# Chunk attention with its probabilities and values as upper and lower fp32r halves, from the fourth row tile on

## The chip, the cores and the metric

The kernel runs on one core of a Trainium2 chip (trn2). The metric is the device time of one execution in microseconds (us). Five engines have in-order instruction streams of their own and meet at semaphores: TensorE (PE: weight loads, PEld, and matmuls), VectorE (DVE), ScalarE (ACT), GpSimd (POOL) and SyncE (SP, which issues loads).

## The reference

Two transformer blocks on 1024 tokens of 1024 channels, fp32. The part that matters is one of three attentions of the second block:

```python
def _chunk_rel(q, k, v, rel_table):        # 4 heads of 64, chunks of 64 rows, 8 chunks to the left
    ...
        kb = lax.dynamic_slice_in_dim(kp, start, BAND, axis=1)
        vb = lax.dynamic_slice_in_dim(vp, start, BAND, axis=1)
        valid = (start - pad + ki) >= 0
        sc = jnp.einsum('bqhd,bkhd->bhqk', qc, kb, preferred_element_type=jnp.float32) * scale
        sc = jnp.where(valid, sc + bias[None], -jnp.inf)
        p = jax.nn.softmax(sc, axis=-1).astype(vb.dtype)
        return jnp.einsum('bhqk,bkhd->bqhd', p, vb)
```

## The kernel before

Products are made in one of two ways. In most of them each fp32 operand is split into an upper half rounded to fp32r and a lower half (the rest), and three fp32r matmuls are added up: helper lines L495 to L497. The products of probabilities and values, and the transposes, are plain fp32 matmuls.

**Chunk attention.** Eight row tiles i of 128 rows, four heads h each: 32 heads in a row, numbered x = 4i + h, in a software pipeline of iterations `it` (`class Heads`, `class Chunked`). Row tile i sees min(i+1, 5) key blocks of 128, so 128, 256, 384, 512 and then always 640 keys. In iteration `it`, in this order,
- PE computes the scores of head `it` (fp32r, keys in two halves, L2963), transposes the probabilities of head `it`-2 (one fp32 matmul against the identity for each key block, L2977; blocks 0 to 3 go to one PSUM bank, block 4 to the other of two "turn" banks, 4 and 5, which are handed out in turn), and multiplies the transposed probabilities of head `it`-3 with the values (L2989, one fp32 matmul for each key block, 64 columns of output, into bank 6 or 7).
- ACT copies its share of transposed groups of head `it`-2 from PSUM (`copy_turned`, L3023), then makes the exponential of head `it` with its sum (L3045); where `it`-3 is the last head of a row tile, it squares that tile's output for a later normalization (L3061).
- DVE copies its share of the transposed groups (L3021), adds the bias to the scores and takes the extreme of each row (negated, so it is a minimum, L3109), and at the end of a row tile takes the reciprocal of the sums (L3077), multiplies them onto the value sums in PSUM (L3081), and one iteration later scales the normalized output (L3125), for which POOL has made the root (L577, L570).

`claim` makes PE wait until the engine that reads a PSUM bank has released it. `turns_by_dve(x, g)` says which of DVE and ACT copies group g of head x: for odd x DVE takes the first group and ACT the second, for even x the other way round. The transposed probabilities and the row tile outputs sit in SBUF: two buffers `pt2` (heads x and x+2 share one), one buffer `o2`.

**The values.** Eight tiles of 128 tokens x 256 channels, `cv`. Five are computed ahead of the stage (`CV_EARLY`), three inside it, in iterations 0 to 2, by 24 fp32r matmuls each; ACT copies each from PSUM (`cv_copy_act`, L3176). ACT also rounds the next stages' weights (L455, `send_to`) in iterations 3 and 6. Behind the stage comes the narrow projection, 24 fp32r matmuls of 420 columns for each of eight token tiles.

## Time and profile before

| | |
|---|---|
| runs of the kernel before | 2338.84 us median of 3 (2338.25 to 2340.36) |
| the profiled execution | 2341.6 us, span 2339.8 us |
| TensorE clock granted | 0.997 of full |
| chunk attention | 1110.9 to 1176.0 us from the span's start |

Times in the timeline are from the span's start. "Idle before <- X" names what ended an idle stretch. Matmul records overlap, since each lasts until its last column has left the array: what a matmul costs in a row of them is the distance of the starts. An fp32 matmul shows as two records. In the profile fp32r matmuls are written "f32" as well.

### The profile page before, as it was taken

What the parts mean: (1) busy time and instruction counts of PE and PEld (TensorE: products, weight loads), DVE (VectorE), ACT (ScalarE), POOL (GpSimd) and SP (SyncE); (2) the same over time, 40 slices, a digit from 0 to 9 for tenths busy, and PEclk for the clock granted to TensorE, in tenths of its full rate; (3) what the DMA queues carried; (4) which work ended last, traced back from release to release, by engine and by line L of the source; (5) the groups of instructions that cost most, each with busy time, mean ns of one, the idle gap of its engine ahead of it and who ended that gap; (6) DMA issues with size and microseconds to landing.
All of it is one profiled execution on the core that took longest, in us unless ns stands there. A gap on an engine that the chain in (4) does not pass through costs nothing. (4 is left out here: it accounts for less than half of the span.)

```text
span 2339.8 us, 30722 instructions
## 1 busy us (share of the span) xinstructions
PE 2303.4 (98%) x11602; PEld 1943.8 (83%) x11602; DVE 1427.8 (61%) x2217; ACT 967.7 (41%) x1965; POOL 863.9 (37%) x733
## 2 busy tenths in 40 slices
PE   9999999999999999999999999999999999999998
PEld 8788888888888888888998877888888888888887
DVE  7999924955454577775533767153494545447776
ACT  4126534533332345455635655134453233234543
POOL 2000125388787800032113121122338878770002
PEclk9999999999999999999999999999999999999999
DMA  5222124233233368664002100243223323336865
GB/s 158 52 63 77 51 90 131 86 117 117 86 117 104 117 243 284 212 215 120 19 19 70 46 5 19 64 154 126 87 67 117 117 86 117 104 120 247 285 214 191
DMA packets 219444, 275.84 MB, mean 118 GB/s; under 512 B 17243, under 2 KB 144956, under 8 KB 216482
## 3 DMA queue, kind: packets, MB, share of 16 engines
q1 hardware_dynamic: 200594, 210.57, 29.0%
q10 hardware_dynamic: 18704, 63.32, 6.9%
q8 instruction: 92, 1.51, 0.3%
q14 instruction: 54, 0.44, 0.1%
HBM read 205.27 MB, written 68.57 MB: 117 GB/s over the span
## 5 line engine op out<-in xcount | busy, mean ns | idle before, releaser
L495 PE MATMUL P<-ah,wh 128*128 128x512 f32 (+1 forms) x1136 | 441.4, 389 | 0.2 <-DVE al L525 0.2
L497 PE MATMUL P<-ah,wl 128*128 128x512 f32 (+1 forms) x1136 | 439.1, 387 | 0.0
L496 PE MATMUL P<-al,wh 128*128 128x512 f32 (+1 forms) x1136 | 439.0, 386 | 0.0
L495 PE MATMUL P<-wh,ah 128*128 128x512 f32 (+2 forms) x1128 | 425.8, 377 | 0.0
L497 PE MATMUL P<-wh,al 128*128 128x512 f32 (+2 forms) x1128 | 423.6, 376 | 0.0
L496 PE MATMUL P<-wl,ah 128*128 128x512 f32 (+2 forms) x1128 | 423.2, 375 | 0.0
L577 POOL TENSOR_TENSOR stats<-stats,epsc 128x1 f32<-128x1 f32 x78 | 32.6, 417 | 773.0 <-ACT xn L1895 421.0
L495 PEld LDWEIGHTS P<-ah,wh 128*128 128x128 f32 x1136 | 213.5, 188 | 43.3 <-issue 0.4
L497 PEld LDWEIGHTS P<-ah,wl 128*128 128x128 f32 x1136 | 213.4, 188 | 43.4
L496 PEld LDWEIGHTS P<-al,wh 128*128 128x128 f32 x1136 | 213.6, 188 | 42.2
L497 PEld LDWEIGHTS P<-wh,al 128*128 128x128 f32 x1128 | 212.3, 188 | 36.5
L496 PEld LDWEIGHTS P<-wl,ah 128*128 128x128 f32 x1128 | 212.4, 188 | 36.3
L495 PEld LDWEIGHTS P<-wh,ah 128*128 128x128 f32 x1128 | 212.4, 188 | 36.2
L461 POOL TENSOR_TENSOR wl<-stage,wh 128x1024 fp32r<-128x1024 f32 (+3 forms) x43 | 99.3, 2316 | 303.1 <-ACT wh L455 302.8
L2819 POOL TENSOR_TENSOR wl<-ws,wh 128x512 fp32r<-128x512 f32 x154 | 203.9, 1346 | 3.0
L2819 POOL TENSOR_TENSOR wl<-stage,wh 128x512 fp32r<-128x512 f32 x128 | 181.5, 1433 | 49.9 <-DVE al L525 34.5
L2352 ACT ACTIVATE wh<-ws 128x512 fp32r<-128x512 f32 x160 | 96.5, 627 | 193.8 <-POOL ws L2812 189.4
L1188 DVE SCALAR_TENSOR_TENSOR acc<-hp,cwt,acc 128x1024 f32<-128x1024 f32 (+1 forms) x142 | 153.1, 1120 | 1.3
L2504 ACT ACTIVATE ah<-rf 128x512 fp32r<-128x512 f32 x154 | 95.7, 622 | 66.4 <-DMA rf<-ff_rows 63.6
L2712 DVE TENSOR_TENSOR al<-rf,ah 128x512 fp32r<-128x512 f32 x154 | 105.6, 686 | 18.7 <-ACT ah L2504 18.4
L455 ACT ACTIVATE wh<-stage 128x1024 fp32r<-128x1024 f32 (+2 forms) x68 | 68.8, 1015 | 78.0 <-PE P L497 49.6
L2352 ACT ACTIVATE wh<-stage 128x512 fp32r<-128x512 f32 x132 | 79.8, 621 | 45.3 <-PE P L497 30.2
(362 smaller groups left out, 4303.2 us busy)
## 6 DMA issues: line engine op xcount, KB each, us to landing
rf<-ff_rows SPq DMA_DIRECT2D x154, 256.0 KB, 5.4
stage<-in_w_down_dram SPq DMA_DIRECT2D x110, 256.0 KB, 3.8
ff_rows<-sb ACTq DMA_DIRECT2D x22, 1024.0 KB, 5.0
stage<-in_w_gu_dram SPq DMA_DIRECT2D x44, 512.0 KB, 5.2
stage<-in_w_in_dram SPq DMA_DIRECT2D x22, 512.0 KB, 4.0
stage<-in_w_gate_dram SPq DMA_DIRECT2D x22, 512.0 KB, 4.6
stage<-in_w_up_dram SPq DMA_DIRECT2D x22, 512.0 KB, 5.1
ff_rows<-uo ACTq DMA_DIRECT2D x22, 512.0 KB, 3.0
```

The source lines that it names most:

```text
L455: e.activation(WH[n % RING][:, 0:plan[n][0]], stage[place(n)][:, 0:plan[n][0]], ACT.Copy).then_inc(*wh.up(n))
L461: port.e.tensor_tensor(WL[n % RING][:, 0:w], stage[place(n)][:, 0:w], WH[n % RING][:, 0:w].bitcast(F32), ALU.subtract).then_inc(*sig.up(n))
L495: e.matmul(out, lh, rh, start=start, stop=False, skip_group_check=onto)
L496: e.matmul(out, lh, rl, start=False, stop=False, skip_group_check=onto)
L497: return e.matmul(out, ll, rh, start=False, stop=stop, skip_group_check=onto)
L577: PL.e.tensor_tensor(v, s, more, ALU.add).then_inc(*rs.up((key, "v")))
L1188: e.scalar_tensor_tensor(dst, src, cwt[:, c, w:w + 1], dst, ALU.mult, ALU.add).then_inc(*tap.up(key))
L2352: AC.e.activation(hi, src, ACT.Copy).then_inc(*wh.up((self.name, (m, op))))
L2504: AC.e.activation(self.rows_place(u)[0], RF[b][:, :], ACT.Copy).then_inc(*ah.up((self.name, "split", u)))
L2712: DV.e.tensor_tensor(lo, RF[self.row_buffer(u)[0]][:, :], hi.bitcast(F32), ALU.subtract).then_inc(*al.up((self.name, "split", u)))
L2819: PL.e.tensor_tensor(lo, src, hi.bitcast(F32), ALU.subtract).then_inc(*wl.up((self.name, (m, op))))
```

## The change

- The values are kept in eight tiles `cv0` to `cv7` of [128, 4, 128]: for each head 64 columns of upper halves (ACT's copy, rounded to fp32r) and 64 of lower ones (`cv_low_dve`: DVE subtracts the upper half from PSUM). PE's bank for a value tile is released by DVE (`al`) instead of ACT (`cp`).
- From head 12 on (row tile 3), the first group of transposed probabilities (key blocks 0 to 3) is kept as an upper half, copied by ACT (`pt_hi`), and a lower half, subtracted by DVE after ACT's copy (`pt_lo`). PE's turn bank is released by DVE's subtraction. The group of the fifth key block is always copied by ACT, in fp32.
- A split key block is multiplied by two fp32r matmuls: upper probabilities with both value halves (128 columns), lower probabilities with the upper value half (64 columns). A block that isn't split is one fp32 matmul as before, but with both value halves (128 columns). So the value sums of each head are 128 wide: upper part and lower part.
- At the end of each row tile DVE copies the lower sums from PSUM to `o`, adds the upper ones, and multiplies by the reciprocal: three instructions, each waiting for the one before, where there was one.
- For split heads DVE's order in an iteration is: extreme of head `it`, then the subtraction for head `it`-2 (before: the copy first).

```diff
+        def turned_signal(self, x, g):
+            return ev if self.split(x, g) or self.turns_by_dve(x, g) else cp
+
+        def value_block(self, out, x, h, kb, k, last):
+
+            e = PE.e
+            if not self.split(x, kb - kb % 4):
+                v = self.halves(h, k).bitcast(F32) if self.stacked(x // 4) else self.v(h, k)
+                return e.matmul(out, self.pt(x, kb, 1)[:, 0, :], v, start=kb == 0, stop=last)
+            hi, lo, both = self.pt_hi(x, kb, 1)[:, 0, :], self.pt_lo(x, kb, 1)[:, 0, :], self.halves(h, k)
+            if kb == 0:
+                e.matmul(out, hi, both, start=True, stop=False)
+            ins = e.matmul(out[:, 0:self.dv], lo, both[:, 0:self.dv], start=False, stop=False, skip_group_check=True)
+            if kb:
+                ins = e.matmul(out, hi, both, start=False, stop=last)
+            return ins
...
-                        claim(b, ev if self.turns_by_dve(x, g) else cp, (self.kind, "pt", x, g))
+                        claim(b, self.turned_signal(x, g), (self.kind, "pt", x, g))
...
-                        ins = e.matmul(P[:, b, self.dv * h:self.dv * h + self.dv], self.pt(x, kb, 1)[:, 0, :],
-                                       self.v(h, k0 + kb), start=kb == 0, stop=kb == nb - 1)
+                        ins = self.value_block(P[:, b, n * h:n * h + n], x, h, kb, k0 + kb, kb == nb - 1)
...
+                halved = self.split(x, g)
+                if not halved and (port is DV) != bool(self.turns_by_dve(x, g)):
                     continue
...
+                if halved and port is DV:
+                    DV.wait_ge(cp, (self.kind, "pt", x, g))
+                    DV.e.tensor_tensor(self.pt_lo(x, g, w), src, dst.bitcast(F32), ALU.subtract).then_inc(
+                        *ev.up((self.kind, "pt", x, g)))
+                    continue
...
-                if 2 <= it <= self.n + 1:
+                halved = 2 <= it <= self.n + 1 and self.split(it - 2, 0)
+                if 2 <= it <= self.n + 1 and not halved:
                     self.copy_turned(DV, it - 2)
                 self.turned_dve(it - 1)
                 if it < self.n:
                     self.maximum(it)
+                if halved:
+                    self.copy_turned(DV, it - 2)
...
+                    if self.stacked(i):
+                        both = P[:, 6 + i % 2, :].rearrange("p (h y d) -> p h y d", h=self.nh, y=2)
+                        e.tensor_copy(o, both[:, :, 1, :]).then_inc(*sm.up((self.kind, "lower", i)))
+                        DV.wait_ge(sm, (self.kind, "lower", i))
+                        e.tensor_tensor(o, both[:, :, 0, :], o, ALU.add).then_inc(*sm.up((self.kind, "sum", i)))
+                        DV.wait_ge(sm, (self.kind, "sum", i))
+                        src = o
+                    e.tensor_tensor(o, src, rden.unsqueeze(2).to_broadcast([128, self.nh, self.dv]),
                                     ALU.mult).then_inc(*ev.up((self.kind, "o", i)))
...
+    def cv_low_dve(t):
+        DV.wait_ge(cp, ("cv", t))
+        DV.e.tensor_tensor(cv[t][:, :, 64:128], P[:, cv_bank(t), 0:256].rearrange("p (h d) -> p h d", h=4),
+                           cv[t][:, :, 0:64].bitcast(F32), ALU.subtract).then_inc(*al.up(("cv", t)))
...
+        upper = [big(f"pt2h_{i}", [128, 4, 128], 57.5 + 2.5 * i, F32R) for i in range(2)]
+        lower = [big(f"pt2l_{i}", [128, 4, 128], 2 + 2 * i, F32R) for i in range(2)]
...
+        def split(self, x, g):
+            return x >= 12 and g == 0
+
+        def turns_by_dve(self, x, g):
+            return x < 12 and x % 2
...
+        def turned_dve(self, it):
+            if CV_EARLY <= CV_EARLY + it < NT:
+                cv_low_dve(CV_EARLY + it)
```

## Rows read from the trace of the kernel before

**Rows 1.** The page, busy time (us), share of the span and instructions of an engine.

```profile
PE 2303.4 (98%) x11602; PEld 1943.8 (83%) x11602; DVE 1427.8 (61%) x2217; ACT 967.7 (41%) x1965; POOL 863.9 (37%) x733
```

**Rows 2.** Windows: span, then busy us of PE, PEld, DVE, ACT, POOL; clock, DMA.

```profile
1120.70:1140.00 19.30, 18.39 (x143) 16.71 (x142) 13.70 (x46) 14.88 (x44) 6.82 (x8) 1.00 0.20 56
1140.00:1171.20 31.20, 31.20 (x266) 31.12 (x266) 20.82 (x55) 19.34 (x50) 2.70 (x8) 1.00 0.01 1
```

**Rows 3.** Timeline of PE, one full iteration: start us, us, engine, line, operation.

```profile
1144.28 0.83 PE L2963 MATMUL P<-ck,cqs 128*128 128x320 f32 x4
1144.95 0.71 PE L2977 MATMUL P<-ident,s 128*128 128x128 f32 x5
1145.49 1.23 PE L2989 MATMUL P<-cv,pt 128*128 128x64 f32 x10
1146.53 0.83 PE L2963 MATMUL P<-ck,cqs 128*128 128x320 f32 x4
```

**Rows 4.** Timeline of PE's weight loads around three fp32r matmuls of 128 columns.

```profile
1267.03 0.19 PEld L2966 LDWEIGHTS P<-causal_r,ident_r 128*128 128x128 f32 x1
1267.14 0.19 PEld L2963 LDWEIGHTS P<-fk,fqs 128*128 128x128 f32 x1
1267.25 0.19 PEld L495 LDWEIGHTS P<-ah,wh 128*128 128x128 f32 x1
```

**Rows 5.** Timeline of PE in latent attention, whose values are 128 columns wide.

```profile
1459.99 1.95 PE L2989 MATMUL P<-mv,pt 128*128 128x128 f32 x16
1461.78 0.38 PE L2977 MATMUL P<-ident,p 128*128 128x128 f32 x2
```

**Rows 6.** Groups by form, ACT and DVE: busy us, mean ns, idle before.

```profile
L3023 ACT ACTIVATE pt<-P 128x512 f32<-128x512 f32 x10 | 5.7, 575 | 0.0
L3023 ACT ACTIVATE pt<-P 128x128 f32<-128x128 f32 x10 | 2.7, 266 | 1.6 <-PE P L2977 1.6
L525 DVE TENSOR_TENSOR al<-P,ah 128x512 fp32r<-128x512 f32 x72 | 47.0, 685 | 32.2 <-ACT ah L517 32.2
L525 DVE TENSOR_TENSOR al<-P,ah 128x256 fp32r<-128x256 f32 x16 | 6.8, 423 | 13.3 <-ACT ah L517 13.2
```

**Rows 7.** Timeline of ACT, DVE and POOL at the end of row tile 4.

```profile
1151.26 0.83 ACT L3045 ACTIVATE s<-s,stats 128x640 f32<-128x640 f32 x1 [0.56 <-DVE stats L3109]
1151.35 0.42 DVE L3081 TENSOR_TENSOR o<-P,stats 128x256 f32<-128x256 f32 x1
...
1152.00 0.19 ACT L3045 ACTIVATION_READ_ACCUMULATOR s<-s,stats 128x1 f32 x1
1152.09 0.40 ACT L3061 ACTIVATE yc<-o 128x256 f32<-128x256 f32 x1
...
1152.39 0.19 ACT L3061 ACTIVATION_READ_ACCUMULATOR yc<-o 128x1 f32 x1
...
1152.93 0.55 POOL L570 TENSOR_TENSOR stats<-stats,nhalf 128x1 f32<-128x1 f32 x1
1152.94 0.81 DVE L3109 CUSTOM_DVE_ANT_0 s<-P,b 128x640 f32<-128x640 f32 x1
...
1153.68 0.08 DVE L3109 DVE_READ_ACCUMULATOR2_ANT stats<- 128x1 f32 x1
1153.68 0.48 DVE L3125 SCALAR_TENSOR_TENSOR yc<-o,stats,gout 128x256 f32<-128x256 f32 x1
```

**Rows 8.** Timeline of PE and ACT in row tiles 0 to 3.

```profile
1121.28 0.40 ACT L3045 ACTIVATE s<-s,stats 128x128 f32<-128x128 f32 x1 [0.46 <-DVE stats L3109]
...
1122.78 0.44 PE L2989 MATMUL P<-cv,pt 128*128 128x64 f32 x2 [0.62 <-ACT pt L3023]
...
1124.98 1.04 ACT L455 ACTIVATE wh<-stage 128x1024 fp32r<-128x1024 f32 x1
...
1126.57 0.44 PE L2977 MATMUL P<-ident,s 128*128 128x128 f32 x2 [0.28 <-ACT s L3045]
...
1137.27 1.00 PE L2989 MATMUL P<-cv,pt 128*128 128x64 f32 x8
```

**Rows 9.** Timeline of PE in the last iterations.

```profile
1173.23 0.77 PE L2977 MATMUL P<-ident,s 128*128 128x128 f32 x5 [0.17 <-ACT pt L3023]
```

## What the change will do to the time

> **What bounds the kernel now.** I read the page's busy shares first: TensorE (PE) is busy 98% of the span [rows 1]. Chunk attention takes some 65 us of it. The table by stage shows PE with no idle time from 1140.0 to 1171.2 and 0.9 us of it in the 19.3 us of the narrow tiles before, while VectorE (DVE) is busy 20.8 and ScalarE (ACT) 19.3 of 31.2 us [rows 2]. So a microsecond more or less on PE's path here is one in the total; work on DVE and ACT is free until PE waits for it.
>
> The timeline of PE shows what a full iteration is made of [rows 3]: scores 0.67 us (1144.28 to 1144.95), five transposes 0.54, values 1.04 for ten records, 2.25 together (1144.28 to 1146.53). An fp32 value matmul is two records, so a record takes 104 to 112 ns. "A record" below is a weight load and its matmul.
>
> **What the change does to PE.** Before, 120 value blocks were 240 records. After, the 80 split blocks are two fp32r records each and the 40 others two fp32 records each: 240 again. The question is what a narrow record costs.
> - The moving side does not set it: fp32 values 128 wide in latent attention take 1.79 us for 16 records (1459.99 to 1461.78), 112 ns each [rows 5], like those 64 wide here. So the 40 unsplit blocks, now 128 wide, cost nothing more.
> - The load sets it, for fp32r too: where three fp32r matmuls only 128 wide follow each other, their weight loads start at 1267.03, 1267.14 and 1267.25, 0.11 us apart [rows 4].
>
> I take 112 ns for an fp32r record: change on PE 0. The bounds: 167 ns, what an fp32r score 320 wide takes (0.67 us for four, [rows 3]), would be 55 x 160 = +8.8 us; the low bound is an estimate of 60 ns, a load half as long with a little on top, 52 x 160 = -8.3 us.
>
> The Trainium skill speaks against my value. "TensorE: Matmul & The Clock Gate", Weight-path perf modes, says that fast weight load is on for 128 weights of a type other than FP32, at about twice the speed. If fp32r counted as such, the loads would be halved. By that rule the stage would win what the first rival below says. The trace does not agree: its fp32r loads keep 0.11 us.
>
> **What it does to ACT and DVE.** ACT copies 128x512 in 0.57 and 128x128 in 0.27 [rows 6]; its exponential of 640, the read of the sum with it, takes 0.92 (1151.26 to 1152.19), DVE's minimum with its read 0.82 (1152.94 to 1153.76) [rows 7]. The lower half (transposed probabilities minus the upper ones, PSUM in, fp32r out) is costed by the same form in row passes, 0.69; for 128x256 it is 0.42 [rows 6]. Overlap with the next instruction makes each some 0.08 shorter in a queue; a semaphore costs 0.03 to 0.05.
> - Per head from row tile 3 on, ACT has both copies (about 1.75 us with the exponential), DVE a minimum and a subtraction (1.43). Both fit into 2.25.
> - A new chain: transposes of head x, upper copy, subtraction, and only then may PE transpose head x+1 into the same bank (five key blocks use both turn banks for each head). From the first transpose: 0.60 to the signal (0.71 for five, 0.11 less for four, [rows 3]), 0.62 and 0.73 for copy and subtraction with their semaphores, 0.05 back to PE: 2.00. PE comes back after 2.25. It fits by some 0.25, if both engines are free.
> - Per row tile, DVE finishes the output by a copy of the lower sums, an addition and a multiplication, each waiting for the one before, where it had one multiplication (0.42, [rows 7]). Two more of 0.42 and 0.03: 0.90 us later. Bounds 0.30 (an SBUF source) and 0.48 (the scaling of the same size, [rows 7]) for each. Behind it on DVE wait the next head's minimum and the subtraction; on ACT the square waits for the output, and **behind the square the next head's upper copy**. The old order had cover for one multiplication, not for three.
>
> **A regular tile, walked.** Time from the start of PE's iteration that ends row tile i; T is the head whose transposes come there. T's upper copy 1.30 to 1.87; DVE's minimum 0.87 to 1.69; subtraction 1.91 to 2.60. Value sums ready 2.41. Reciprocal 2.52; copy 2.73; addition 3.18; multiplication 3.63 to 4.05. ACT: square 4.09, free at 4.49; upper copy of T+1 (transposed by 3.52) 4.49 to 5.06. DVE: minimum until 4.79, subtraction 5.10 to 5.79. PE wants to transpose T+2 at 4.49 + 0.67 = 5.16, and can at 5.84: it stalls **0.68 us**. One iteration on, DVE's scaling (its root comes 0.9 us after the square's read, 1152.58 to 1153.48 in [rows 7]) and a minimum end at 6.93, upper copy of T+2 at 7.04, subtraction 7.77, PE due at 8.09: caught up. Nothing accumulates.
>
> **The sum.**
> - In iteration 3 the lower half of the eighth value tile (0.42, in a queue 0.34) goes before the minimum of head 3, for which ACT's exponential is waiting [rows 8]; ACT's next copy is what PE stalls for at 1122.78: +0.34.
> - Row tile 0: PE is idle before 1126.57 for the exponential, which stood behind the square and the 1.04 us weight rounding of 1124.98 [rows 8]; the square is 0.90 later: +0.90.
> - Row tiles 1 and 2: tile 1's 0.90 is mostly covered (0.2 left, but DVE enters tile 2 0.4 late). In tile 2 the iterations are short (1.6 to 1.9 us). From the start of iteration 14 (1132.86, some 0.06 late): DVE's minimum until 1.79; ACT, behind the late exponential of head 13, the upper copy of head 12 until 2.37; its subtraction until 3.10; reciprocal, copy, addition, multiplication until 4.55; square; upper copy of head 13 until 5.56, its subtraction until 6.29, PE at 6.34: the value matmuls of head 13, at 1137.27 before [rows 8], start at 1139.20, +1.93 for both tiles.
> - Row tile 3: as the regular tile, but the iteration has one value block less, so PE is back 0.21 earlier: +0.89.
> - Tiles 4 and 5: 2 x 0.68 = +1.36.
> - Tile 6 and the end: there are no scores left in the iteration that stalls, so PE is back 0.64 earlier, and the last heads run at the chain's own pace. Before, PE idled 0.17 there [rows 9]. Walked to the last value matmul: +1.65. Tile 7's output has the 4.6 us of the next stage's first tile as cover.
> - The other five or so subtractions for value tiles lie under PE's token matmuls: 0.
>
> Sum 7.1 us; PE 0. No DMA moves, no queue of SP or POOL gets anything. Against the profiled execution 2341.6 + 7.1 = 2348.7; that one lies 2.8 above the median of the runs shown, so the forecast is 2338.8 + 7.1 = **2345.9 us**, 0.30% slower. What a measurement can tell from no change is 0.2%, 4.7 us: from 2334.2 to 2343.5.
>
> **Rivals.**
> 1. *Narrow fp32r records at 60 ns instead of 112* (the other side). 8 x 52 ns = 0.42 a head. With five blocks the chain of 2.00 allows only 0.25 of it, 16 heads: 4.0; in tile 3 it is 4 x 0.42 = 1.7. Sum -5.7, net +1.4: 2340.2, not slower. It decides from a saving of 2.4 us, some 0.12 a head. For it: the moving part of 64 or 128 columns is far shorter than 112 ns. Against: the loads of that very type in [rows 4]. 8%, of which 3 end under -0.2% (only if the chain is shorter too). The skill's rule above is this rival.
> 2. *The output chain is covered better*: each added operation 0.30 instead of 0.45 makes every one of seven stalls 0.3 shorter, 7.1 - 2.1 = 5.0; with tile 1 fully covered and the first stall lost in ACT's own waits 7.1 - 3.5 = 3.6: 2342.4, no measurable change. For it: PE's slack of 0.25 an iteration can take back what ACT is late. Against: the regular walk leaves no doubt of order, since all three engines are in order. 20%.
> 3. *The chain does not fit*: semaphores and ACT's fifth-block copy make it 2.45 instead of 2.00. Then PE loses 0.2 in each of 15 iterations and never recovers in a tile: 7.1 + 3.0 = 10.1, 2348.9. For it: the margin is thin beside so many summed durations. Against: each handover in the trace is 0.03 to 0.05. 13%.
> 4. *Narrow fp32r is dearer on PE*, up to the 167 ns bound: up to 7.1 + 8.8 = 15.9, 2354.7. [rows 4] speak against it. 5%.
>
> My forecast (stalls of 5 to 9 us in all): 54%.
>
> **Numbers.** Slower by over 0.2%: 54 + 13 + 5 = 72. Same: rivals 1 and 2 less the fast end, 25. Faster: 3. The range of 2341.0 to 2350.5 takes in rivals 2 and 3 and leaves out rival 1, rival 4 and a few in 100 beyond rival 3's sum; the forecast's own is 2343.5 to 2348.
>
> **What the changed profile would show.** Right: the value matmuls of a head still ten records in about 1.04 us, fp32r loads 0.11 apart; PE idle in front of a transpose, released by DVE's subtraction, once per row tile for 0.5 to 0.9 us and between them none; over 1 us before the values of head 13; ACT's square waiting for DVE's output and the upper copy directly behind it; the next stage starting some 7 us later. Wrong: value groups of 0.6 us (rival 1), idle PE in every iteration (rival 3), value groups over 1.2 us (rival 4), stalls under 0.4 us (rival 2).

## The result, and the profile after

| | before | after |
|---|---|---|
| median of 6 runs | 2339.36 us (2338.25 to 2340.67) | 2351.42 us (2349.41 to 2355.11) |
| ratio | | 1.0052, 95% interval 1.0042 to 1.0062 |
| profiled execution, span | 2341.6, 2339.8 us | 2349.41, 2347.3 us |

The change makes the kernel 12.1 us slower. 7.1 was forecast; the sign is right, the time lies above the range (2350.5).

The page of after, busy times. Beside [rows 1] DVE has 26 and ACT 18 instructions more, PE exactly as many records as before.

```profile
PE 2304.7 (98%) x11602; PEld 1941.6 (83%) x11602; DVE 1442.4 (61%) x2243; ACT 973.4 (41%) x1983; POOL 864.8 (37%) x733
```

The windows of after, same columns as [rows 2]. PE, without idle time from 1140.0 to 1171.2 before, now has 2.3 us of it, and 2.2 in the narrow tiles, where it had 0.9. (The windows don't cover the same heads to the microsecond: after enters the stage 2.4 us earlier.) The last one has no counterpart in the chunk stage of before: a stretch at clock 0.50, 1.2 GHz where the rows around it are at 2.4.

```profile
1120.70:1140.00 19.30, 17.11 (x123) 14.68 (x124) 15.14 (x47) 13.71 (x39) 6.68 (x8) 1.00 0.20 55
1140.00:1171.20 31.20, 28.92 (x240) 27.93 (x238) 24.34 (x54) 21.38 (x58) 2.22 (x6) 1.00 0.01 2
...
1179.40:1186.20 6.80, 6.80 (x31) 6.71 (x29) 2.05 (x5) 1.07 (x3) 0.00 (x0) 0.50 0.00 0
```

The timeline of after, the iteration that ends row tile 4 and the one behind it (all engines but the weight loads). It is the walk of the prediction, in the order that it had.

```profile
1150.95 0.83 PE L2988 MATMUL P<-ck,cqs 128*128 128x320 f32 x4
...
1152.26 0.60 ACT L3054 ACTIVATE pt2h<-P 128x512 fp32r<-128x512 f32 x1 [0.68 <-PE P L3002]
...
1152.99 0.69 DVE L3048 TENSOR_TENSOR pt2l<-P,pt2h 128x512 fp32r<-128x512 f32 x1 [0.33 <-ACT pt2h L3054]
...
1153.20 0.83 PE L2988 MATMUL P<-ck,cqs 128*128 128x320 f32 x4
1153.60 0.17 DVE L3111 RECIPROCAL stats<-stats 128x4 f32<-128x4 f32 x1
...
1153.80 0.42 DVE L3119 COPY o<-P 128x256 f32<-128x256 f32 x1
...
1154.26 0.43 DVE L3121 TENSOR_TENSOR o<-P,o 128x256 f32<-128x256 f32 x1
...
1154.72 0.42 DVE L3124 TENSOR_TENSOR o<-o,stats 128x256 f32<-128x256 f32 x1
...
1155.18 0.42 ACT L3092 ACTIVATE yc<-o 128x256 f32<-128x256 f32 x1 [1.34 <-DVE o L3124]
...
1155.60 0.58 ACT L3054 ACTIVATE pt2h<-P 128x512 fp32r<-128x512 f32 x1
...
1156.27 0.69 DVE L3048 TENSOR_TENSOR pt2l<-P,pt2h 128x512 fp32r<-128x512 f32 x1 [0.39 <-ACT pt2h L3054]
...
1157.02 0.66 PE L3002 MATMUL P<-ident,s 128*128 128x128 f32 x4 [0.73 <-DVE pt2l L3048]
```

The iteration itself still takes 2.25 us (1150.95 to 1153.20), as in [rows 3]. The output now is a chain of three (1153.80 to 1155.14); the square waits for it, the upper copy stands behind the square, the subtraction behind that, and PE idles in front of the transposes: 0.73 us here, 0.82 at 1147.07 and 0.73 at 1166.97 behind the row tiles before and after. The same timeline over the stage, PE's other long stalls:

```profile
1125.38 0.44 PE L3002 MATMUL P<-ident,s 128*128 128x128 f32 x2 [0.58 <-ACT s L3076]
...
1138.16 0.33 PE L2967 MATMUL P<-cv,pt2h 128*128 128x128 f32 x1 [1.10 <-DVE pt2l L3048]
...
1176.91 0.77 PE L3002 MATMUL P<-ident,s 128*128 128x128 f32 x5 [1.31 <-DVE pt2l L3048]
...
1179.08 1.08 PE L3002 MATMUL P<-ident,s 128*128 128x128 f32 x5 [0.29 <-DVE pt2l L3048]
```

The last line is in the half-clock stretch, so its five transposes show 1.08 us. To size the terms I use a second profile of the changed kernel, *again* below, which has no such stretch in or behind the stage.

**Lags.** "Lag" below is how much later a row starts than its counterpart before, both counted from the start of the scores of head 1 (1113.97 us before, 1111.77 in again). Example: the next stage's first transposes start at 1185.46 before and 1193.38 in again, so the lag is 81.61 - 71.49 = 10.12 us.

### The profile page after: what moved, and what is told of

It is laid out like the page before. It is cut to its first block and busy times, and to the rows that moved or that the text cites. A ratio compares the mean times of both kernels' runs of the same rounds, so it can differ in the third digit from the quotient of the medians.

```text
span 2347.3 us, 30788 instructions
## 1 busy us (share of the span) xinstructions
PE 2304.7 (98%) x11602; PEld 1941.6 (83%) x11602; DVE 1442.4 (61%) x2243; ACT 973.4 (41%) x1983; POOL 864.8 (37%) x733
## 5 line engine op out<-in xcount | busy, mean ns | idle before, releaser
L1188 DVE SCALAR_TENSOR_TENSOR acc<-hp,cwt,acc 128x1024 f32<-128x1024 f32 (+1 forms) x142 | 153.1, 1120 | 1.3
```

The costliest lines, as they stand in the source:

```text
L1188: e.scalar_tensor_tensor(dst, src, cwt[:, c, w:w + 1], dst, ALU.mult, ALU.add).then_inc(*tap.up(key))
```

## The experiments

The medians are of 5 runs each, of 11 for one_mult, values_only and no_lower_probs and of 7 for clear. All were timed beside runs of the kernel before on the same chip. "Over before" is against the median of those runs: 2339.72 for again, one_mult, values_only and no_lower_probs; 2338.42 for square_late, both_orders, tail_fill and fixed; 2338.30 for spread, early_loads, all_three and busy_wait; 2338.70 for clear and square_clear. These four groups ran on four chips, so kernels of different groups are compared by this column. The lags are those of one profiled execution each, half-clock stretches included.

| kernel | median us | over before | ratio, 95% interval | lag at last values / next stage's transposes |
|---|---|---|---|---|
| again | 2351.78 | 12.1 | 1.0050 (1.0038 to 1.0063) | 8.89 / 10.12 |
| one_mult | 2343.57 | 3.9 | 1.0015 (1.0006 to 1.0023) | 3.11 / 3.29 |
| values_only | 2343.44 | 3.7 | 1.0014 (1.0006 to 1.0023) | 1.99 / 3.22 |
| no_lower_probs | 2337.97 | -1.8 | 0.9994 (0.9985 to 1.0003) | -4.35 / -3.11 |
| square_late | 2349.60 | 11.2 | 1.0047 (1.0034 to 1.0059) | 9.94 / 10.87 |
| both_orders | 2351.81 | 13.4 | 1.0058 (1.0044 to 1.0071) | 11.43 / 13.35 |
| tail_fill | 2351.41 | 13.0 | 1.0053 (1.0041 to 1.0066) | 8.98 / 9.91 |
| fixed | 2352.68 | 14.3 | 1.0058 (1.0046 to 1.0071) | 10.34 / 11.30 |
| spread | 2348.76 | 10.5 | 1.0042 (1.0028 to 1.0056) | 7.07 / 8.20 |
| early_loads | 2349.89 | 11.6 | 1.0050 (1.0038 to 1.0063) | 8.88 / 9.15 |
| all_three | 2347.15 | 8.8 | 1.0036 (1.0023 to 1.0049) | 7.54 / 7.49 |
| busy_wait | 2352.81 | 14.5 | 1.0058 (1.0045 to 1.0071) | 10.79 / 12.81 |
| clear | 2345.14 | 6.4 | 1.0027 (1.0016 to 1.0037) | 5.21 / 5.15 |
| square_clear | 2349.83 | 11.1 | 1.0040 (1.0026 to 1.0053) | 6.74 / 7.77 |

### Which part costs: again, one_mult, values_only, no_lower_probs

**again** is the changed kernel unaltered.

> The changed kernel once more, unchanged, for a second profile. Theory A (three parts: the output's two more DVE instructions with the square and the next upper copy queued behind them stall PE for about 8.6 us in chunk attention; PE's records cost nothing more; and the idle stretches let TensorE's clock fall to its lower level at the stage's end, which costs some 3 us more): the time is 2351 plus or minus 2 and follows the clock: PE's idle time in the stage is again 8 to 9 us, and what differs between the two profiles is how long the clock is at half. Theory B (no clock part; 12 us are all waits that one profile doesn't show rightly): idle time in the stage near 12 us.

It repeats the result: +12.1 us. The lag in the stage is 8.89 us with no half-clock stretch there, so theory B (12 us of waits in the stage) is out. Whether idle PE brings the clock down is not shown by this run.

**one_mult** takes the output from the upper sums alone, one multiplication as before; it leaves the products with the lower value halves out of the result.

```diff
-                        e.tensor_copy(o, both[:, :, 1, :]).then_inc(*sm.up((self.kind, "lower", i)))
-                        DV.wait_ge(sm, (self.kind, "lower", i))
-                        e.tensor_tensor(o, both[:, :, 0, :], o, ALU.add).then_inc(*sm.up((self.kind, "sum", i)))
-                        DV.wait_ge(sm, (self.kind, "sum", i))
-                        src = o
+                        src = both[:, :, 0, :]
```

> The row tile's output is made by one multiplication of the upper sums, as before; the copy and addition of the lower sums are left out, so the lower halves of the values don't reach the output. Theory A: DVE's output is 0.93 us earlier. By the same walk that leaves 0.34 for the last value tile, about 0.5 in tile 2, under 0.1 in a regular tile and 0.9 at the end: 2341 to 2342, and no stretch at half clock at the stage's end. Rival (the chain of upper copy and subtraction in every iteration, or narrow fp32r records, is what costs): 2347 or more, with PE idle in front of transposes in iterations that end no row tile.

2343.57: 8.2 us less than again, 2 us more than expected. Without the two added operations of DVE on eight row tiles, 0.9 us each, two thirds of the cost are gone. Lag before the transposes of head 7 (their row is [rows 8], 1126.57): 0.33, where again has 1.24. These are the 0.34 and 0.90 of the sum, each within a hundredth; but half of the second shows one wait earlier than forecast, at the values of head 5, which wait 0.35 us for DVE's copy (lag 0.84 there).

**values_only** halves no probabilities: the values stay split and the output is made in three steps.

```diff
         def split(self, x, g):
-            return x >= 12 and g == 0
+            return False
         def turns_by_dve(self, x, g):
-            return x < 12 and x % 2
+            return (x + g // 4) % 2
```

> Only the values are kept in halves: the probabilities are never split, so every value product is one fp32 matmul 128 columns wide, DVE and ACT share the copies as before, and the output still takes three instructions. Theory A: the three instructions are needed for the stall but not enough; without the subtraction behind ACT's copy PE has a copy's time more. Left are 0.34, the 0.9 of tile 0 and some 0.5 in tiles 1 and 2: about 2341.2. Rival 1 (the output chain alone costs it): 2347 or more. Rival 2 (fp32 matmuls 128 wide cost more than 64 wide, 240 records): at 10 ns each 2.4 us more, and value groups of five blocks longer than 1.04 us.

The waits of PE in it, 1120 to 1180 us (us in total, times, longest): none stands in row tiles 3 to 6.

```profile
PE P L2964 <- ACT pt L3054: 0.6, 1, 0.6
PE P L3002 <- ACT s L3076: 0.6, 1, 0.6
PE P L2964 <- DVE pt L3052: 0.4, 1, 0.4
PE P L3002 <- ACT pt L3054: 0.3, 1, 0.3
```

So the three steps do nothing by themselves once iterations are 2.25 us long (lag 1.62 to 1.65 from head 17 to head 26), and the halves do little there (one_mult: 1.40 to 1.62 over the same heads). Only together do they stall PE in the regular tiles, as the walk has it; each of them, taken away alone, takes 8.2 or 8.3 us off again.

**no_lower_probs** makes and multiplies no lower probability halves: 80 records, DVE's subtractions and their products are left out of the result.

```diff
-            if kb == 0:
-                e.matmul(out, hi, both, start=True, stop=False)
-            ins = e.matmul(out[:, 0:self.dv], lo, both[:, 0:self.dv], start=False, stop=False, skip_group_check=True)
-            if kb:
-                ins = e.matmul(out, hi, both, start=False, stop=last)
-            return ins
+            return e.matmul(out, hi, both, start=kb == 0, stop=last)
...
```

> The lower halves of the probabilities are left out: no subtraction by DVE, the turn bank is released by ACT's upper copy, and a split block is one fp32r matmul of 128 columns instead of two, 80 records fewer; the output still takes three instructions. If a record costs 112 ns (theory A): 9.0 us of PE's work go, of which some 1.3 are lost because ACT then needs about 1.85 us an iteration; stalls at the row tiles' ends stay near 0.9: about 2344. If a narrow fp32r record costs 60 ns: 4.8 us go, 2346.6. If the subtraction is what stalls PE, the stalls go too: 2337 or less.

A full iteration in its timeline, six value records instead of ten:

```profile
1151.82 0.83 PE L2983 MATMUL P<-ck,cqs 128*128 128x320 f32 x4
1152.49 0.71 PE L2997 MATMUL P<-ident,s 128*128 128x128 f32 x5
1152.95 0.64 PE L2966 MATMUL P<-cv,pt2h 128*128 128x128 f32 x4
1153.43 0.44 PE L2964 MATMUL P<-cv,pt 128*128 128x128 f32 x2
```

Four split blocks go from 1152.95 to 1153.43, 0.12 us a record. 80 records less at 0.11 are 8.8 us. The loss at the last values falls by 13.2 (8.89 to -4.35), the other 4.4 being stalls that went with the subtraction. My main forecast kept those stalls: 2344, where 2337.97 came out; the last alternative of the three had them go. It also shows that the record price decides nothing between before and after: an fp32r record, with its load, is as dear as half an fp32 matmul.

### The order: square_late, both_orders, tail_fill, fixed

**square_late** puts ACT's square of row tile i one iteration later, behind the next head's upper copy.

```diff
-                if it >= 3 and self.at(it - 3)[1] == self.nh - 1:
+                if self.kind != "chunk" and it >= 3 and self.at(it - 3)[1] == self.nh - 1:
                     self.square(self.at(it - 3)[0])
...
+                if self.kind == "chunk" and it >= 4 and self.at(it - 4)[1] == self.nh - 1:
+                    self.square(self.at(it - 4)[0])
...
```

> The same arithmetic, all of it; only ACT's square of a row tile's output is moved behind the next iteration's upper copy, so that the copy doesn't wait for DVE's output. Theory A: the upper copy is over at 4.15 instead of 5.2 after the iteration's start, but the subtraction still stands behind the next minimum, until 5.6: the stall of a regular tile falls from 0.93 to about 0.5, tile 2's from 1.9 to 1.3: some 2.5 us less in all, and what the clock gives back, 2346 to 2349. Rival (the queue order on ACT doesn't matter, DVE's work does): 2351.

**both_orders** adds to it that DVE, in the first iteration of each row tile, does the subtraction before the minimum.

```diff
+                first_now = halved and it % 4 == 3
-                if 2 <= it <= self.n + 1 and not halved:
+                if 2 <= it <= self.n + 1 and (not halved or first_now):
                     self.copy_turned(DV, it - 2)
...
-                if halved:
+                if halved and not first_now:
                     self.copy_turned(DV, it - 2)
```

> The same arithmetic. ACT's square behind the next upper copy, and in the iteration after a row tile's last one DVE makes the subtraction before the minimum. Theory A: subtraction over at 4.97 after the iteration's start, PE due at 5.16: no stall in the regular tiles. Left are 0.34, tile 0's 0.9 or less, some 0.5 in tile 2 and 1 at the end: 2341.5 to 2343, with the clock at full at the stage's end. Rival (DVE has too much work in all): stalls move to the next minimum and exponential, 2346 or more.

The regular stall falls from 0.95 to 0.48 with the square alone (lags 7.03, 7.50, 7.99 at heads 18, 22, 26), and to about 0.65 with both: what is no longer in front of the copy is in front of the exponential, which waits for the later minimum and has the next upper copy behind it. But neither kernel is measurably faster, since both gain a stall of 2.2 us in row tile 1. Both forecasts were missed, that of both_orders (2341.5 to 2343) by 9 us. The timeline of both_orders shows it:

```profile
1124.65 2.35 POOL L461 TENSOR_TENSOR wl<-stage,wh 128x1024 fp32r<-128x1024 f32 x1
1124.71 2.56 DVE L3171 SCALAR_TENSOR_TENSOR yc<-o,stats,gout 128x256 f32<-128x256 f32 x1 [0.80 <-POOL stats L570]
...
1127.20 0.55 DVE L3155 CUSTOM_DVE_ANT_0 s<-P,b 128x384 f32<-128x384 f32 x1
...
1127.80 0.78 PE L2988 MATMUL P<-ck,cqs 128*128 128x384 f32 x2 [2.22 <-DVE stats L3155]
```

DVE's scaling, 0.48 us in [rows 7], takes 2.56 because POOL's subtraction began 0.06 us before it; it ends 0.27 after POOL's. The moved square moved the root, and the root let both start together. I tested this with the last two kernels below.

**tail_fill** takes the first half of the next stage's first token tile into the last three iterations, where PE idles. **fixed** is both_orders with it.

```diff
+            if it in NAR_EARLY:
+                nar_steps(NAR_EARLY[it])
...
+    NAR_EARLY = {31: range(0, 2), 32: range(2, 3), 33: range(3, 4)}
...
```

> The orders are those of the changed kernel. Four of the eight steps (12 of 24 matmuls) of the next stage's first token tile are made in PE's last three iterations of chunk attention, where it idles 1.3 and 0.3 us and waits for the last head. Theory A with the clock: the 2.1 us of waits in the end go, and with them most of the time at half clock behind it: 2346 to 2348. If the clock falls anyway, from the waits before: about 2349.5 with a stretch at half clock in the profile. Rival (no clock part): 2349.3.

> Both new orders and the filled end together, all arithmetic kept. Theory A: left are 0.34, up to 0.9 in tile 0 and 0.5 in tile 2, less 0.2 that the kernel before idles at the end: 2340 to 2341.5, not to be told from the kernel before, since PE's work is the same. If narrow records were dearer than before: 2343 or more. If they were cheaper: 2337 or less.

Neither gained, and fixed misses its forecast by 11 us; it has the 2.2 us stall of row tile 1 as well. In tail_fill the moved products fit into the stalls (lag 8.98 at the last values), but the lag at the next stage's transposes is 9.91 against 10.12: PE has the first token tile ready earlier and waits 3.33 us for DVE. So PE's own work at the end of the stage does not set what comes next; the next section finds what does.

### The next stage: early_loads, spread, all_three

Timeline of SP's queue and DVE behind the stage, in again:

```profile
1186.42 0.30 DVE L3618 MEMSET tt<- 128x128 f32 x2 [0.16 <-DVE yc L3166]
...
1188.10 0.33 SPq L3514 DMA_DIRECT2D causal<-in_c_causal_dram  x1
...
1192.04 0.19 DVE L3637 TENSOR_TENSOR ra<-P,ropek 128x32 f32<-128x32 f32 x1 [3.49 <-DMA causal<-in_c_causal_dram]
...
1193.38 0.63 PE L3536 MATMUL P<-ident,tt 128*128 128x128 f32 x4 [1.34 <-issue]
```

SP issues five small loads only when the scaling of row tile 7 has ended the chunk stage; DVE needs all five, and PE needs DVE. The last load is issued at 1180.49 before and 1188.10 in again: 9.81 of lag, 0.9 more than the last values have. From there to DVE's first instruction on what was loaded it is 3.63 us before and 3.94 in again, the other 0.3. Before, PE's matmuls idled 0.04 us there and its weight loads 0.37, in again 1.34 and 1.66.

**early_loads** issues three of the five (ropek, fbias, causal) ahead of the chunk stage.

```diff
+        e.dma_start(fbias[0:4, :], I["f_bias_2"][0].rearrange("(n a) -> n a", a=1)).then_inc(*l_nar.up("fbias"))
+        e.dma_start(causal[:, :], I["c_causal"]).then_inc(*l_nar.up("causal"))
+        e.dma_start(ropek[:, :, :], I["c_ropek"]).then_inc(*l_nar.up("ropek"))
         load_to(first["fv"] + 2)
...
```

> The changed kernel; three of the five small loads that the next stage's first token tile waits for (bias, mask, rotation table) are issued before chunk attention instead of behind its end. Theory: the 1.3 us that PE idles before the next stage's first transposes hang on the last of these loads, which start only when DVE has ended chunk attention, now 0.9 us later; with two loads instead of five behind it the idle time is under 0.2 us: 1.1 us less than the changed kernel, 2350.5. Rival (the idle time is instruction fetch or ACT's and POOL's work on the first tile): it stays 1.3 us, 2351.6.

The lag at the last values stays (8.88), that at the transposes falls from 10.12 to 9.15, PE's wait from 1.34 to 0.37. The 1.0 us is there in the trace; in the times over before (11.6 against 12.1, the five runs from 2348.23 to 2353.93) it can't be told from the spread of the runs.

**spread** deals the output's steps out: copy of the lower sums in the iteration where it stood, addition and multiplication one iteration later around the subtraction, square and scaling later by the same.

```diff
+                if self.kind == "chunk" and it >= 7 and it % 4 == 3:
+                    self.output_sum((it - 7) // 4)
                 if halved:
                     self.copy_turned(DV, it - 2)
+                if self.kind == "chunk" and it >= 7 and it % 4 == 3:
+                    self.output_scaled((it - 7) // 4)
...
```

> All arithmetic of the changed kernel; the three output instructions are dealt out over two iterations of DVE: reciprocal and lower copy at the end of a row tile's last iteration, addition between the next minimum and subtraction, multiplication behind that subtraction; ACT's square then behind that iteration's exponential, and the scaling one iteration later. Theory A (in-order queues: what stalls PE is not the amount of DVE's work but that 0.9 us of it lie in one piece in front of the next minimum, subtraction and upper copy): each piece fits a gap of some 0.4 us, the regular tiles don't stall. Left are 0.34 in iteration 3, a few tenths in tiles 0 and 2, and the end as in the changed kernel (2.4 in the stage, 1.2 before the next stage's first transposes): some 4.5 us over the kernel before, 2344 to 2346. Rival (DVE and ACT have too much work in all, so the wait only moves, as it did where the square and the subtraction changed places): 2349 or more.

**all_three** is spread, tail_fill and early_loads in one.

> Output instructions dealt out, the end filled with the next stage's matmuls, and the three loads early; all arithmetic kept. Theory A: 0.34 and a few tenths in tiles 0 to 2 are left, less 0.4 that the kernel before idles before those transposes and 0.2 at its end: 2340 to 2341.5, not to be told from the kernel before, since PE has the same records. If fp32r value records were cheaper than fp32 ones, 2337 or less; if the wait moves again, 2345 or more.

In spread the regular stall is gone: lag 5.66 at head 17, 5.75 at head 27, where again goes from 3.51 to 6.53. That shows the walk from the other side: with the same work and the same records, the stalls of row tiles 3 to 6 vanish when no upper copy stands behind a chain of three. But here, too, PE stalls 2.17 us in row tile 1, as in both_orders; spread misses its forecast by 3 us and all_three by 6.

### The overlap of DVE and POOL: clear, square_clear

ACT's rounding of the weights of iteration 6 is moved to iteration 7, and POOL's subtraction behind it, so that the subtraction begins after DVE's scaling. **clear** is all_three with this, **square_clear** square_late with it.

```diff
-        sends = {3: first["narrow"] + 3, 6: first["fv"]}
+        sends = {3: first["narrow"] + 3, 7: first["fv"]}
...
-                    low_to(self.sends[3 + 3 * i])
+                    low_to(self.sends[3 + 4 * i])
```

> All three rearrangements as before, and ScalarE's rounding of the weights of iteration 6 (and with it GpSimd's 128x1024 subtraction behind it) moved to iteration 7, so that GpSimd's subtraction starts after VectorE's scaling of row tile 0. If the overlap is what costs (theory): the scaling takes 0.48 again, the idle 2.17 us before the values at 1128.6 go to 0.3 or less, and the time falls by 2.0 to 2.2 from 2347.15, to 2344.5 to 2345.5, without half-clock stretches inside the stage 2342 to 2344. If the scaling takes long for its own sake, or the idle time only moves to the next wait (rival): 2346.5 to 2347.5, with 1.5 us or more of idle TensorE elsewhere in row tiles 1 and 2.

> The square one iteration later, as before, with the same move of the rounding from iteration 6 to 7. Theory: the 2.22 us of idle TensorE before the scores of head 10 are gone, 2.0 to 2.2 less than 2349.60: 2347.4 to 2347.8. Rival (the scaling is long for its own sake): 2349 to 2350.

Timeline of clear, DVE and POOL in row tile 1:

```profile
1125.47 0.48 DVE L3185 SCALAR_TENSOR_TENSOR yc<-o,stats,gout 128x256 f32<-128x256 f32 x1 [1.00 <-POOL stats L570]
1125.56 2.63 POOL L461 TENSOR_TENSOR wl<-stage,wh 128x1024 fp32r<-128x1024 f32 x1
```

The scaling is at 0.48 again; now POOL's, 0.09 us behind, takes 2.63 instead of 2.35, which nobody waits for. clear comes to 2345.14, 6.4 us over before where all_three has 8.8, and is the fastest kernel with the whole change. The lag at the transposes of head 13 falls from 4.32 to 1.56; 1.7 of it is a half-clock stretch that all_three had there, from 1129.0, right behind the stall, and clear has not, about 1.0 the overlap, since a new wait of 1.32 us for ACT's copy at 1125.81 gives half of the gain back. That wait is the rival's, in part. In square_clear the lag behind the same stall, at the transposes of head 8, falls from 3.32 to 1.49, and at those of the next stage from 10.87 to 7.77; its scaling, too, takes 0.48. The median does not follow (2349.83 in 5 runs from 2345.67 to 2350.05): so wide a spread hides 2 us, and this test is in the trace only.

What clear still loses, 5.15 of lag: 1.6 up to the transposes of head 13, 1.5 more up to those of head 17, 0.1 from there to head 29, 2.0 from there to the next stage, where DVE now waits for the two loads that were left behind the stage.

### The clock: busy_wait

**busy_wait** computes the scores of heads 16, 20, 24 and 28 a second time, in the iterations in which PE stalls.

```diff
+                    twice = self.kind == "chunk" and it >= 16 and it % 4 == 0
-                    for w in range(0, W, size):
+                    for w in [*range(0, W, size)] * (2 if twice else 1):
```

> The changed kernel; in four iterations in which PE waits 0.7 to 1.1 us right behind the scores (heads 16, 20, 24, 28) the scores are computed twice into the same bank, 0.6 us of PE work each, so some 2.4 us of idle PE are filled with work that nobody needs. The waits themselves keep their ends. If the clock falls because PE idles in the stage: fewer or no stretches at half clock there, mean clock 0.998 and up to 2 us less than the changed kernel, 2349.5 to 2350.5. If idle time in the stage doesn't matter for the clock: 2351.5 to 2352, clock 0.997.

2352.81, with a mean granted clock of 0.996: the extra products did not keep the clock up. Its profile has the longest stretch at half clock of all, 10.2 us from 1181.6, right behind the stall that is left (1.32 us at 1179.5). So nothing here shows that filling the stalls keeps the clock; it isn't shown either that the stalls have no part in it, since the longest one remained.

The other traces speak for a part of the stalls. In the sixteen profiles ten half-clock stretches begin between 1120 and 1195 us. One begins in an idle time of PE of 2.34 us (all_three, 1190.4), each of the others within 2.5 us behind the end of a stall of 1.1 to 3.4 us. All five kernels with the 2.2 us stall in row tile 1 have one there, from 1128.1 to 1130.0, and none of the eleven other profiles has. But stalls as long also passed at full clock, 1.32 and 1.34 us in again and 2.34 in clear, and before has its three stretches far from this stage. So a stretch often follows a long stall and need not; no run isolates the cause.

## Why the prediction was wrong

The direction, the mechanism and its places were right. The sum, 7.1 us, was 5.0 short: 1.8 in stalls that were sized too small, 1.2 at a wait that it put at nothing, 2.0 outside the lags. In the terms of the prediction, measured by the lags of again:

| term | forecast | measured |
|---|---|---|
| PE's records | 0 | 0 |
| iteration 3 and row tile 0 | 0.34 + 0.90 | 1.24 |
| row tiles 1 and 2, to the values of head 13 | 1.93 | 2.07 |
| row tile 3 | 0.89 | 1.24 |
| row tiles 4 and 5 | 2 x 0.68 | 0.96 + 0.95 |
| row tile 6 and the end | 1.65 | 2.43 |
| in the stage | 7.07 | 8.89 |
| next stage | 0 | 1.23 |
| the rest | 0 | about 2.0 |

- **PE's price: right.** The ten value records of a head go from 1152.09 to 1153.20 in after, 1.11 us where I said 1.04, but the transposes ahead of them 0.47 instead of 0.54, so that the iteration stays at 2.25. The halves' loads keep 0.11 us, as read from [rows 4]; timeline of again:

```profile
1182.03 0.19 PEld L2970 LDWEIGHTS P<-cv,pt2h 128*128 128x128 f32 x1
...
1182.14 0.19 PEld L2968 LDWEIGHTS P<-cv,pt2l 128*128 128x128 f32 x1
...
1182.26 0.19 PEld L2970 LDWEIGHTS P<-cv,pt2h 128*128 128x128 f32 x1
```

  Rivals 1 and 4 fall, and rival 2 with them: the addition takes 0.43 and the multiplication, from SBUF, 0.42, not 0.30. The Trainium skill's rule on fast weight load ("TensorE: Matmul & The Clock Gate", Weight-path perf modes) would have had them at about half; for fp32r the measurement decides against it.
- **The regular tile: the chain was right, its handovers were not.** From the start of the iteration at 1150.95: upper copy 1.31 (walked 1.30), but 0.60 long, not 0.57, and the subtraction starts 0.13 behind its end, not 0.04. So it ends at 2.73 instead of 2.60, and all DVE does behind it is 0.13 late: output ready at 4.19 (4.05). Square and next upper copy give 0.03 more, the second handover 0.06: subtraction until 6.01 (5.79), PE at 6.07 (5.84). Stall 0.91 to 0.96 instead of 0.68. The step that failed is the term "0.62 and 0.73 for copy and subtraction with their semaphores", and with it rival 3's "each handover in the trace is 0.03 to 0.05". The trace of before has the same handover, ACT's rounding copy to DVE's subtraction, at 0.03 (300.59 + 0.60 = 301.19 to 301.22), in all 34 cases in which DVE sat idle for it:

```profile
300.59 0.60 ACT L517 ACTIVATE ah<-P 128x512 fp32r<-128x512 f32 x1 [0.26 <-PE P L507]
301.22 0.69 DVE L525 TENSOR_TENSOR al<-P,ah 128x512 fp32r<-128x512 f32 x1 [0.16 <-ACT ah L517]
```

  What differs is the number of waits. That subtraction has one `wait_ge`; the new one has three, two of them for events that ACT's copy has waited for already:

```python
                port.wait_ge(tp, (self.kind, x, g))
                if x >= 2:
                    port.wait_ge(pv, (self.kind, x - 2))
                ...
                    DV.wait_ge(cp, (self.kind, "pt", x, g))
```

  In the trace of after 14 of the subtractions carry three waits and start 0.13 behind the copy, 5 carry two and start 0.10 behind it. The trace of before had such handovers too, behind other lines: 0.13 for both DVE instructions with three waits that ACT released (1766.89 to 1767.02), 0.10 for six of nine with two, 0.03 for all 92 with one. So the number was there to be read. No run leaves the two waits out. In all, the terms inside the stage come out 1.8 us short, the largest part (0.8) at the end, where the heads run at the chain's own pace.
- **Rival 3** (the chain doesn't fit) had the same cause with a larger size, but the wrong consequence: in a plain head the subtraction ends 2.06 us behind the first transpose (1151.62 to 1153.68; 1.95 was walked), and the next transposes come after 2.25 (1153.87): it fits. From row tile 3 on PE idles for over 0.2 us in no iteration but those behind a row tile's end and the last ones.
- **"Tile 7's output has the 4.6 us of the next stage's first tile as cover": failed, a term put at nothing.** I followed only the products. The stage's end, later by the output's 0.9 us, also releases five loads of SP, DVE waits for the last of them, and PE for DVE: 1.23 us. The chain was in the trace of before, as a wait of 2.20 us of DVE for the load of causal (until 1184.12) with PE's weight loads idle for 0.37 us behind it (until 1185.43), and early_loads shows it by taking 1.0 us of it away.
- **The rest goes with the clock for the most part; its cause is open.** The lag at the next stage is 10.1 us, the difference of the medians 12.1. Nothing behind it costs more: from the next stage's first transposes to the end of the span it is 1152.75 us in after, 1152.80 in again and 1154.33 in before, whose profile has a half-clock stretch of 3.4 us there. The mean granted clock of the 11 runs of after and again is 0.9969, that of the 56 runs of before beside the experiments 0.9981: 0.0012 of 2340 us are 2.8 us, an estimate that would be enough for what is left. At equal clock the kernels are 10.75 us apart (0.998: five changed runs with median 2349.41, 21 of before with 2338.66), which leaves 0.6 that no trace here places; the clock is given to 0.001 only. No run shows what makes the changed kernel's clock lower; the traces point to its stalls (busy_wait, above). In after it is the 6.8 us stretch from 1179.4, behind the stalls of 1.31 and 0.29, which put the lag at the transposes at 11.53 instead of 10.12.
- **The comparison by single profiles** would have hidden this. The two profiled executions differ by 7.8 us, near the forecast of 7.1. That is luck: the one of before stood 2.8 above the median of the runs shown, its part up to the scores of head 1 was 2.4 us longer and its part behind the next stage's first transposes 1.6 (it had three half-clock stretches of 3.4 us, two in the first part and one in the second), while the lag between the two is 11.5.

The range failed with it: its upper end lay 1.6 us above rival 3's sum, and had no room for a term outside the stage or for the clock.

## What to carry to other kernels

Walk the order of each engine behind an added operation, not only its duration: 0.9 us on an engine that is 61% busy cost as much on the one that is 98% busy, because an in-order square stood between it and the copy that PE needed; dealing the same steps out over two iterations took those stalls away. Count the waits of the instruction behind a handover, and look up in the trace what a handover with as many takes: 0.03 us with one and 0.13 with three, once per head, is what the walk sized too low. At the end of a stage, follow what its end releases (loads of the next stage, semaphores of every engine) before you call a later end covered. When something moves in time by half a microsecond, ask what it will now run beside: here that stalled PE for 2.2 us in five kernels, and in three of them (square_late, both_orders, fixed) the lag at the last values came out larger than again's.

## What the runs showed of the hardware

- **A DVE operation with two operands in SBUF beside a POOL operation**: 0.48 us alone, 2.56 beside a POOL subtraction of 2.35 us begun 0.06 us earlier; with DVE 0.09 us ahead, DVE 0.48 and POOL 2.63. The later of the two waits for all of the other. The Trainium skill states this ("SBUF — State Buffer", SBUF: two separate sides): DVE and GpSimd share a port pair, an exclusive lock that whoever starts first holds for its whole instruction, where DVE's instruction has two SBUF inputs and GpSimd's reads SBUF. The trace agrees.
- **A record with its weight load takes 0.11 us in fp32r too, 64 or 128 columns alike.** Halving the columns of such a record gains nothing; what gains is one record less (no_lower_probs: 0.12 a record in 1152.95 to 1153.43, four blocks in 0.48 us, where two records a block take 0.21 in [rows 3] and 0.22 in after).
- **What a DVE instruction takes to start behind ACT's goes with the number of semaphores it waits for**: 0.03 us with one (92 of 92 in before), 0.13 with three (1152.86 to 1152.99 in after, 14 of the 14 subtractions), also where the other events had come long before; with two it was 0.10 in all five subtractions (1156.18 to 1156.27) and in six of the nine other cases of before.
- **Half-clock stretches of 3.4, 6.8 and 10.2 us** (clock 0.50) stand at different places in different executions, of the same kernel too (after, again), and cost up to half their length: the one from 1129.0 in all_three raised the lag from 2.61 at the values of head 7 to 4.33 at the transposes of head 10. In and right behind the chunk stage they came with or shortly behind stalls of PE of over 1 us. A difference of 2 us in 2340 can't be read from one execution of each kernel.
